# Expert rows gathered one block further ahead, expert weights read from the arrays as given

## The reference

```
idx, gates = top_4(h @ w_router + b_router)      # 512 x 4 assignments, grouped by expert
for each block of at most 128 rows of one expert e:
    gu   = xblk @ w_gate_up[e] + b_gate_up[e]    # [rows, 1024] @ [1024, 2048]
    gate = min(gu[:, :1024], 7);  up = clip(gu[:, 1024:], -7, 7)
    act  = (up + 1) * gate * sigmoid(1.702 * gate)
    y    = act @ w_down[e] + b_down[e]           # [rows, 1024] @ [1024, 1024]
out[token] += gate_weight * y[row]               # four rows per token
```

## Time and profile before

| | us |
|---|---|
| median of 3 runs (lowest, highest) | 3572.2 (3571.51, 3579.55) |
| the profiled execution: time / span | 3570.16 / 3568.2 |
| PE busy | 3138.1 (88%) |
| expert stage: first weight load issued | 798.2 |
| first transposes of gathered rows, PE | 810.7 to 812.7 |
| end of the last down projection, PE | 1928.4 |

### The profile page before, as it was taken

One profiled execution on the slowest core, in us unless ns is written; L12 is line 12 of the kernel. 1 busy time (PEld: TensorE's weight loads), 2 busy tenths in 40 slices (PEclk: granted clock), 3 DMA queues, 4 the chain that ended last, 5 costly groups with the idle time before them and its releaser, 6 DMA issues.

```text
span 3568.2 us, 36838 instructions
## 1 busy us (share of the span) xinstructions
PE 3138.1 (88%) x13316; PEld 1710.1 (48%) x13317; DVE 915.3 (26%) x2214; ACT 753.3 (21%) x1479; POOL 115.9 (3%) x135
## 2 busy tenths in 40 slices
PE   7999989948999899998997588888998788978997
PEld 3454644435585364663575245444444345444443
DVE  3441641131212212122221224122112124041121
ACT  2221631011211212112110114132111215141111
POOL 0000000020000000000000000010000000010000
PEclk9999999958999999999998799999999899999998
DMA  3211012119989999999984120212221210202212
GB/s 127 71 60 47 2 58 77 67 50 393 412 309 406 403 405 378 393 366 408 400 346 172 65 69 16 71 36 79 81 71 53 79 57 14 83 24 89 77 65 77
DMA packets 111778, 575.26 MB, mean 161 GB/s; under 512 B 14046, under 2 KB 21726, under 8 KB 85953
## 3 DMA queue, kind: packets, MB, share of 16 engines
q1 hardware_dynamic: 101808, 556.90, 40.4%
q0 software_dynamic: 9872, 17.08, 1.3%
HBM read 569.91 MB, written 21.05 MB: 166 GB/s over the span
## 4 chain that ended last, share of the span: by engine, by line
PE 78%; DMA 9%; DVE 6%; issue 2%; ACT 2%; DVEq 1%; POOL 1%; SPq 0%; POOLq 0%; ACTq 0%; PEldq 0%
PE banks L317 39%; PE banks L1148 11%; PE banks L1126 9%; PE banks L314 6%; DMA arena<-h_rows,arena 4%; PE banks L1101 3%; PE banks L599 2%; PE banks L622 2%; PE banks L610 2%; DMA arena<-in_w_experts 1%; DVE arena L672 1%; DMA arena<-in_w_in 1%; PE banks L1083 1%; PE banks L263 1%; DVE arena L684 1%
## 5 line engine op out<-in xcount | busy, mean ns | idle before, releaser
L317 PE MATMUL banks<-arena 128*128 128x512 f32 (+3 forms) x3328 | 1431.4, 592 | 107.8 <-DMA arena<-in_w_in 54.1
L317 PEld LDWEIGHTS banks<-arena 128*128 128x128 f32 x3328 | 638.9, 193 | 874.6 <-issue 856.9
L1148 PEld LDWEIGHTS banks<-arena 128*128 128x128 f32 x3584 | 403.3, 192 | 15.9 <-issue 15.9
L1148 PE MATMUL banks<-arena 128*128 128x128 f32 x3584 | 405.1, 276 | 6.1 <-issue 6.1
L1126 PE MATMUL banks<-arena 128*64 128x512 f32 (+1 forms) x1024 | 337.4, 625 | 0.0
L1101 PE MATMUL banks<-arena 128*64 128x512 f32 x1152 | 261.8, 605 | 13.8 <-DMA arena<-in_w_experts 11.3
L314 PE MATMUL banks<-arena 128*128 128x512 f32 x512 | 224.8, 601 | 12.0 <-DMA arena<-in_w_in 12.0
L1219 DVE TENSOR_TENSOR arena<-banks,arena 128x512 f32<-128x512 f32 x64 | 44.3, 692 | 735.7 <-PE banks L1148 420.3
L1126 PEld LDWEIGHTS banks<-arena 128*64 128x64 f32 (+1 forms) x1024 | 126.5, 167 | 189.3 <-issue 189.1
L822 DVE TENSOR_TENSOR arena<-banks,arena 128x512 f32<-128x512 f32 x64 | 44.4, 693 | 540.1 <-PE banks L317 540.1
L263 PE MATMUL banks<-arena 128*128 128x128 f32 (+1 forms) x524 | 85.5, 317 | 93.2 <-DVE arena L381 71.0
(11 more groups left out here) (195 smaller groups left out, 1828.5 us busy)
## 6 DMA issues: line engine op xcount, KB each, us to landing
arena<-in_w_experts SPq DMA_DIRECT2D x192, 2048.0 KB, 15.5
arena<-in_w_in SPq DMA_DIRECT2D x84, 1024.0 KB, 4.9
arena<-in_w_out SPq DMA_DIRECT2D x12, 1024.0 KB, 5.0
arena<-in_w_branch SPq DMA_DIRECT2D x24, 512.0 KB, 3.5
arena<-expert_rows SPq DMA_DIRECT2D x4, 2048.0 KB, 14.9
arena<-in_w_in SPq DMA_DIRECT2D x4, 832.0 KB, 7.5
arena<-in_gate_b SPq DMA_DIRECT2D x2, 1536.0 KB, 6.7
arena<-in_x SPq DMA_DIRECT2D x1, 2048.0 KB, 7.8
```

Of the source, the lines that this page charges most:

```text
L317: last = PE.matmul(PS[:, tt, 0:ncols], lhsT(kk, tt), Wh[h][:, q, 0:ncols], start=(kk == 0), stop=(kk == kt - 1))
L1148: last = PE.matmul(PS[:, q, f * P:(f + 1) * P], ch[q][:, k, f * P:(f + 1) * P], xT[:, k], start=(k == 0), stop=(k == 7))
```

## The change

Two parts. First, the expert weights are no longer laid out by the host. `w_gate_up` and `w_down` are read as given: a partition's share of a gate or up chunk is 8 rows of 2 KB (512 of 2048 columns of rows p, 128 + p, ...; 8 KB from one partition to the next, 1 MB from one of the 8 rows to the next), and of a down chunk 4 rows of 4 KB. A chunk is still 2 MB, loaded by one DMA, into the same place in the same order.

```diff
+                    gu = A["w_gate_up"][bass.ds(e, 1)].rearrange("o (k p) f -> p (o k) f", p=P)
+                    dn = A["w_down"][bass.ds(e, 1)].rearrange("o (f p) d -> p (o f) d", p=P)
+                    srcs = [gu[:, :, 0:512], gu[:, :, 1024:1536], gu[:, :, 512:1024], gu[:, :, 1536:2048],
+                            dn[:, 0:4], dn[:, 4:8]]
                     for q in range(6):
 ...
-                        sp.dma_start(v(BIG + 4096 * q, 4096), A["w_experts"][bass.ds(e, 1), q].rearrange("o p n -> p (o n)")).then_inc(SEM[f"ch{q}"], 16)
+                        sp.dma_start(ch[q], srcs[q]).then_inc(SEM[f"ch{q}"], 16)
```

```diff
-                J = MAXBLK + 1
+                J = MAXBLK + 2
 ...
                 V.tensor_copy(tok, column(ALLT, entry(dve, BCOL, 0, LISTS - 1))).then_inc(SEM["tok_rdy"], 1)
+                dve.wait_ge(SEM["gathered"], 16)
+                V.tensor_copy(tok, column(ALLT, entry(dve, BCOL, 1, LISTS - 1))).then_inc(SEM["tok_rdy"], 1)
                 with dve.Fori(0, nb) as j:
 ...
-                    after = entry(dve, BCOL, j + 1, LISTS - 1)
+                    after = entry(dve, BCOL, j + 2, LISTS - 1)
-                    dve.wait_ge(SEM["gathered"], 16 * j + 16)
+                    dve.wait_ge(SEM["gathered"], 16 * j + 32)
 ...
                 next_rows(2)
+                next_rows(3)
                 scatter(1)
                 with pool.Fori(1, nb) as j:
-                    next_rows(j + 2)
+                    next_rows(j + 3)
                     scatter_over(j)
                     scatter(j + 1)
                 scatter_over(nb)
-                pool.wait_ge(SEM["gathered"], nb * 16 + 16)
+                pool.wait_ge(SEM["gathered"], nb * 16 + 32)
```

More of the change, by code:

```diff
@@ L91, in constant_parts @@
         ("iota_e", np.tile(np.arange(NE), (P, 1))),
-        ("iota_j", np.tile(np.arange(MAXBLK + 1), (P, 1))),
+        ("iota_j", np.tile(np.arange(MAXBLK + 2), (P, 1))),
         ("steps", np.tile(np.arange(TOPK) * P, (P, 1))),
@@ L1205, in dve_ @@
                     here = entry(dve, BCOL, j, LISTS - 1)
-                    after = entry(dve, BCOL, j + 1, LISTS - 1)
+                    after = entry(dve, BCOL, j + 2, LISTS - 1)
                     V.tensor_copy(v(BCUR, 16), dyn(BT + e * 16, 16))
-                    dve.wait_ge(SEM["gathered"], 16 * j + 16)
-                    apart(dve, 16 * j + 16)
+                    dve.wait_ge(SEM["gathered"], 16 * j + 32)
+                    apart(dve, 16 * j + 32)
                     V.tensor_copy(tok, column(ALLT, after))
@@ L1276, in pool_ @@
                 scatter_over(nb)
-                pool.wait_ge(SEM["gathered"], nb * 16 + 16)
-                apart(pool, nb * 16 + 16)
+                pool.wait_ge(SEM["gathered"], nb * 16 + 32)
+                apart(pool, nb * 16 + 32)
             return Stage({}, sp=sp_, pe=pe_, act=act_, dve=dve_, pool=pool_)
@@ L1907, in lay_out @@
     m = {k: f[k] for k in ("x", "norm_mix_g", "w_in", "w_proj_a", "w_proj_b", "w_out", "norm_ffn_g", "w_router",
-                           "b_router", "b_down", "w_in_2", "pre_g_2", "post_g_2",
+                           "b_router", "w_gate_up", "w_down", "b_down", "w_in_2", "pre_g_2", "post_g_2",
                            "mla_w_uq_2", "mla_w_ukv_2", "w_branch_2", "w_out_2")}
@@ L1922, in lay_out @@
     m["rel_rows"] = f["ca_rel_bias_2"][:, :, np.minimum(r + P - cc, 128) + 128].reshape(16, P, 256)
-    gate_up = f["w_gate_up"].reshape(NE, 8, P, 4, 512)[:, :, :, [0, 2, 1, 3]].transpose(0, 3, 2, 1, 4)
-    down = f["w_down"].reshape(NE, 2, 4, P, D).transpose(0, 1, 3, 2, 4)
-    m["w_experts"] = cat([gate_up.reshape(NE, 4, P, 4096), down.reshape(NE, 2, P, 4096)], 1)
     m["consts"] = cat([a for _, a in constant_parts()], 1)
```

## The result

The changed kernel takes 3597.46 us (3592.94 to 3604.64, 4 runs) where the one before took 3573.19: a ratio of 1.0071, 95% interval 1.0049 to 1.0094. It is slower by 24 us; 3576 was forecast, in a range of 3547 to 3620. The profiled execution took 3596.89, its span is 3594.9, 26.7 over the one of before.

What follows compares the result with a forecast made beforehand. In the expert stage, PE bounds wide blocks and the weight queue runs of narrow ones. Narrow blocks +2.5 and block 0 +1.4 gave +3.9 on 3570.2, 3574.1; the median stands 2.0 higher: 3576 us, range 3547 to 3620.

Steps and rivals of the forecast that it cites:

- The likeliest case: Expert stage: the gather's gain is paid back to the slower weight queue; 3576 us, own range 3560 to 3590, chance 0.48.
- B: Rival: short weight rows cost more in long streams, below about 388 GB/s; 3608 us at 365 GB/s; chance 0.23.
- Part 1: Gather issued ahead of the scatter: its 30.1 us of waits vanish; worth 25.4 us with the old weight rows.
- DVE's new wait: DVE waits for gather j + 2 at the top of block j; counted as 0, with 1.5 us left.
- The pace: Weight queue with short rows: 398 and 408 GB/s, giving a period of 34.0 us a block, 1.9 more than before.
- the 2.6 for gather and scatter: Weight queue: gathered and scattered rows add 2.6 us a block on the engine that ends last.
- the forecast's own sum: Narrow blocks' waits at a period of 34.0: together 69.6 us against 67.1 before, +2.5.
- The slope of 17 us per microsecond: Expert stage: one microsecond of queue period moves the end by some 17 us, from 14 periods and the starts' chunks.
- A run of narrow blocks after enough wide ones starts with the queue drained: Expert stage: no load backlog at a run's start, so blocks 2-3 and 7-8 wait only 1.6 us each.
- the recurrence: Expert stage: calculation following weight-chunk landings against PE's wanted times through runs of narrow blocks; 112.0 us for blocks 23-26 before.
- A: Rival: short rows cost nothing in a long stream, so only the gather's -25.4 us counts; 3547 us, chance 0.23.
- C: Rival: gathers take 18.5 us and DVE's new wait holds some 12 narrow blocks, 18 us; 3594 us, chance 0.06.

Runs made afterwards that it cites:

- E1: Changed kernel with expert weights back in 16 KB rows, so only the gather moved one block further ahead: 3555.92 us, ratio 0.9956.
- E9: E1 with experts renumbered by the host so that narrow and wide blocks alternate: 3521.07 us, ratio 0.9866.
- E5: Changed kernel with token numbers shifted out of range, so gathers bring almost no rows: 3575.54 us, ratio 1.002.
- E6: Changed kernel with gate and up weights laid out by the host in contiguous chunks read in 4 KB rows: 3576.18 us, ratio 1.0021.
- E2: Kernel before with weights read from the arrays as given, the gather left behind the scatter: 3599.99 us, ratio 1.0086.
- E3: Changed kernel with each gate/up chunk laid out as one contiguous 2 MB piece, still in 2 KB rows: 3605.65 us, ratio 1.0098.
- E8: Kernel reading whole gate/up rows with an early activation table, given contiguous 16 KB down rows and stride-4 weight reads: 3990.17 us, ratio 1.1184.

## Why the prediction was right or wrong

**Direction and size.** The range held, the forecast itself did not: 2.8 us more was forecast, 24 came. The likeliest case said "within 0.3%" (0.38); it is 0.7%, and slower by more than 0.3% had 0.37. The range held because it reached into B, not because the working was right: by the prediction's own signs, B's case has begun. It was to start at a period of 34.4, and 34.42 was measured; blocks 11, 12, 17, 18, 25 and 26 move 381 to 387 GB/s, under its 388. (Worked back from the period, as the forecast did it, the 2 KB rows alone move 8.39 / (34.42 - 2.6 - 10.3), 390.)

**Part 1 held.** All waits for the gather behind block 0 went, DVE's new wait (60.9 us in 32) held up no one, and the gain with long rows is 17 us of median and 21.4 of narrow blocks (E1), where 25.4 was forecast. The 15.5 us taken for the gather are those of one issued right behind the scatter; issued ahead of it, it lands in 10.7 beside 16 KB rows (E9) and in 7.0 beside short ones, so the time to spare was larger than forecast.

**The pace held, nearly.** Period 34.4 instead of 34.0: windows of 3.5 us elsewhere, with the 2.6 for gather and scatter, foretold an unseen stream within 1.2%. Redone with 34.4, the forecast's own sum gives 76.1 in place of 69.6, so this is 6.5 us. The slope of 17 us per microsecond looks right too (from E1 to the changed kernel the narrow blocks grow by 45.8 us for 2.64), but in part by luck: some 9 of the 45.8 are the two starts of the next paragraph, which the slope did not hold.

**The step that failed: "A run of narrow blocks after enough wide ones starts with the queue drained".** It was counted so for blocks 2-3, 7-8 and 23-26. Behind blocks 0 and 1 it isn't: three blocks are 103 us of queue from the first load at 797, so by this estimate block 2's last chunk lands at about 903, in the block that began at 892. The trace agrees: the first down chunk of block 2 was issued at 885.3 and landed 13.6 us later, at 898.9, 7 us into the block. The second was still to follow when the loads of block 3 began at 899.3. At E1's pace of 31.8 the same start held: blocks 2 and 3 took 23.9 each there; at the 33.2 of E5 and E6 they already took 54.0 and 55.6 together. Here blocks 2-3 take 56.2 us, 8.6 beyond 47.6, where 1.6 was forecast. Blocks 7-8, which follow three wide ones, take 3.5 beyond it. Blocks 23-26 stand behind a single wide one and a narrow one; 27.4 came where 22.0 was forecast. Altogether narrow blocks other than the first lie 87.4 beyond 23.8 each, forecast 69.6. Of these 17.8 the period has 6.5, and the two starts have 6.7 and 4.3 beyond what the period adds to them; terms of both signs leave 0.3. Part of the 6.7 is a slower PE behind the wait, which the recurrence had nowhere: in block 3, with a mean granted clock of 0.95, the 16 products behind the last wait take 5.17 us instead of 3.66. At the old pace the assumption had cost little, where blocks 23-26 of before left 2.9 us over that I put down to the clock.

**The rest.** Block 0 took 4.1 us longer than before but began 4.4 earlier, so it ends 0.3 earlier, where 1.4 later was forecast. 6.7 us of the profiled difference lie behind the stage, within what unchanged code scatters. With the 17.8 that makes the 22.8 by which the profiled execution missed its forecast.

**A** (short rows cost nothing in a long stream) fell with E2, **B's** cause with E3, though its price came in part, **C** with the timeline of PE, which has no wait for DVE in this kernel. The mechanism forecast, a gain handed back to the weight queue, is what E1, E2, E5 and E6 show; that the short rows also take away the reason for the gather ahead, by letting it land in 7 to 8 us, I had not seen.

## What to carry to other kernels

Where a stage alternates between two limits, take the period of each from the trace, and then follow the queue through the actual order of the blocks from its first load: "drained" has to be shown, not assumed, and one more microsecond of period may stop it from ever being true. Two changes that act on the same wait are not to be added; here the second alone removed what the first was made for. Before making transfers faster, see whether another order of the work hides them: here it gave 35 us where the gather ahead had given 17.

## What the runs showed of the hardware that I had not expected

A gather of rows issued right behind a scatter lands in 7.7 us beside 2 KB rows (E2) and in 15.3 beside 16 KB rows (before), with the engines equally full. Issued ahead of the scatter, it takes 7.0 (changed kernel) and 10.7 (E9).

SP is held in the issue of a load when the loads have many rows. Issue of weight loads, min/median/max in ns, changed kernel:

```profile
L1076 SPq DMA_DIRECT2D arena<-in_w_gate_up x128: 372/2126/9929, 797.3 to 1890.9; - x128
```

Before, all 192 took 332 to 362 ns. With 4 KB rows (E6) the median of the gate and up loads is 373 and the longest 5212. The prediction had put this at 0.1 us. The chain of the page puts 1% of the span on these issues. Whether they cost time of their own stays open: in the blocks that wait, the engines were full all the while.

A weight load of 128 x 128 whose columns lie 16 bytes apart takes 330 ns instead of 192 (E8), and the products behind it 397 instead of 275.
